# Six changes of order in a one-core decoder block, and its output projection's first weights asked for without the wait for the GDN inverse

## The reference

```
h = rmsnorm(x, g_mix);  proj = h @ w_in                      # GLA q,k,v,gate; GDN conv q,k,v; z; a,b
conv = silu(sum(xc[:, j:j + T] * gdn_conv_w[j] for j in range(4)))        # GDN q,k,v
o_a = gated linear attention(4 heads);   o_b = gated delta rule(8 heads)  # chunked for the prompt
x = x + concat(norm(o_a) * silu(gr), norm(o_b) * silu(z)) @ w_out
m = rmsnorm(mem, g_mem);  k = m @ w_k;  v = m @ w_v                       # memory of 256 rows
s = einsum('bthd,bmhd->bhtm', rmsnorm(x) @ w_q, k) * 512 ** -0.5          # 4 heads of 512
x = x + einsum('bhtm,bmhd->bthd', softmax(s), v) @ w_o                    # samples: cached k, v
x = x + (silu(h @ w_gate) * (h @ w_up)) @ w_down;   y = rmsnorm(x, g_final)
```

## Time and profile before

| | us |
|---|---|
| median of 3 runs | 1809.09 |
| lowest, highest run | 1808.67, 1809.23 |
| the profiled execution | 1807.64 |
| its span in the trace | 1805.9 |
| PE busy | 1766.5 (98%) |
| DVE, ACT, POOL busy | 1090.5, 763.2, 176.4 |

### The profile page before, as it was taken

The page is one execution under the profiler, slowest core; times in us unless marked ns, Lnnn a source line. Parts: engine busy times, 40 slices in busy tenths (PEclk is TensorE's granted clock), DMA queues, the critical chain, the costliest instruction groups (busy, mean ns, idle before and its releaser), DMA issues.

```text
span 1805.9 us, 34933 instructions
## 1 busy us (share of the span) xinstructions
PE 1766.5 (98%) x14223; PEld 1685.6 (93%) x14223; DVE 1090.5 (60%) x1501; ACT 763.2 (42%) x803; POOL 176.4 (10%) x179
## 2 busy tenths in 40 slices
PE   8999999999999999999999999999999999999997
PEld 6999999998999998786679999999999999999997
DVE  6888447756766676553366566665444566665443
ACT  5554546345733533343213444443333444433444
POOL 5000000001055000000015400000000000000231
PEclk9999999999999999999999999999999999999999
DMA  8455545552565679777935788885557888874553
GB/s 271 148 179 187 177 150 163 166 169 82 163 223 178 206 250 326 252 272 253 331 103 178 217 248 244 247 249 157 160 177 212 240 245 247 247 211 138 175 178 113
DMA packets 415130, 367.23 MB, mean 203 GB/s; under 512 B 11519, under 2 KB 374014, under 8 KB 414486
## 3 DMA queue, kind: packets, MB, share of 16 engines
q1 hardware_dynamic: 387368, 340.76, 61.2%
q10 hardware_dynamic: 27678, 25.26, 4.3%
HBM read 347.84 MB, written 18.35 MB: 203 GB/s over the span
## 4 chain that ended last, share of the span: by engine, by line
PE 89%; DVE 5%; ACT 2%; issue 1%; DMA 1%; POOL 1%; DVEq 0%; SPq 0%; ACTq 0%; POOLq 0%
PE ps L478 67%; PE ps L554 9%; PE ps L535 4%; DVE w_lo L457 2%; PE ps L1000 1%; PE ps L521 1%; PE ps L1123 1%; PE ps L1492 1%; ACT w_hi L450 1%; DMA gst<-in_state_gla_dram 1%; PE ps L1527 1%; DVE cacc L647 1%; DMA ring<-in_cache_mem_v_dram 1%; PE ps L1029 0%; PE ps L1536 0%
## 5 line engine op out<-in xcount | busy, mean ns | idle before, releaser
L450 ACT ACTIVATE w_hi<-raw 128x2048 fp32r<-128x2048 f32 (+1 forms) x285 | 512.2, 1797 | 913.6 <-PE ps L478 727.0
L457 DVE TENSOR_TENSOR w_lo<-raw,w_hi 128x2048 fp32r<-128x2048 f32 (+1 forms) x285 | 620.3, 2176 | 300.4 <-ACT w_hi L450 297.2
L478 PE MATMUL ps<-act_hi,w_lo 128*128 128x264 f32 x2560 | 733.9, 287 | 5.6 <-DVE w_lo L457 4.1
L478 PE MATMUL ps<-act_lo,w_hi 128*128 128x264 f32 x2560 | 726.5, 284 | 0.0
L478 PE MATMUL ps<-act_hi,w_hi 128*128 128x264 f32 x2560 | 726.1, 284 | 0.0
L478 PEld LDWEIGHTS ps<-act_hi,w_lo 128*128 128x128 f32 x2560 | 482.8, 189 | 9.6 <-issue 3.8
L478 PEld LDWEIGHTS ps<-act_lo,w_hi 128*128 128x128 f32 x2560 | 483.1, 189 | 0.5
L478 PEld LDWEIGHTS ps<-act_hi,w_hi 128*128 128x128 f32 x2560 | 480.5, 188 | 0.0
L478 PE MATMUL ps<-ff_hi,w_lo 128*128 128x264 f32 x704 | 201.5, 286 | 0.0
L478 PE MATMUL ps<-ff_hi,w_hi 128*128 128x264 f32 x704 | 200.4, 285 | 0.0
L478 PE MATMUL ps<-ff_lo,w_hi 128*128 128x264 f32 x704 | 199.7, 284 | 0.0
(11 more groups left out here) (454 smaller groups left out, 1967.0 us busy)
## 6 DMA issues: line engine op xcount, KB each, us to landing
raw<-in_w_in_dram SPq DMA_DIRECT2D x56, 1024.0 KB, 7.5
raw<-in_ffn_w_gate_dram SPq DMA_DIRECT2D x44, 1024.0 KB, 5.7
raw<-in_ffn_w_up_dram SPq DMA_DIRECT2D x44, 1024.0 KB, 5.7
raw<-in_ffn_w_down_dram SPq DMA_DIRECT2D x32, 768.0 KB, 4.9
raw<-in_ffn_w_down_dram SPq DMA_DIRECT2D x32, 640.0 KB, 6.2
raw<-in_w_out_dram SPq DMA_DIRECT2D x16, 1024.0 KB, 6.9
raw<-in_xa_w_q_dram SPq DMA_DIRECT2D x16, 1024.0 KB, 6.8
raw<-in_xa_w_k_dram SPq DMA_DIRECT2D x16, 1024.0 KB, 7.4
```

Source lines behind the costliest of these rows:

```text
L450: act.activation(w_part(ph, w_hi[b]), raw_part(ph, r, half), ACT.Copy)\
L457: dve.tensor_tensor(w_part(ph, w_lo[b]), raw_part(ph, r, half), w_part(ph, w_hi[b]), ALU.subtract)\
L478: mm = pe.matmul(ps[:, acc(ph, u), 0:ph.cols], w[b][:, k, :], v[:, kk + k, 0:ph.cols], start=first and k == 0 and m == 0, stop=last and k ...
```

## The change

There are seven edits. Six change an order, one takes a wait out.

1. The convolution's taps on DVE: the tap over the samples goes ahead of the one over the prompt, and each waits for its own predecessor, two instructions back.
2. w_out's unit (1, 0) is split in two halves of 8 tiles, each as soon as its part of the buffer is free; on DVE the low halves stand between the takes.
3. PE no longer waits for all takes of w_out ahead of the query projection. (Its first unit has waits of its own, tile by tile from k = 13.)
4. The two squares of the memory rows on ACT stand behind different splits (n = 1, 2), their root behind that of n = 3.
5. The sample queries are turned in the middle of their unit, and ACT copies them ahead of the split of that step.
6. The prompt's values use three accumulator banks instead of two, wait for their own rows of vm only, and the sample rows are turned first; DVE makes the low part of the next weights behind them.
7. SP's first loads of w_out no longer wait for `inv_ready`.

```
@@ new helpers for unit (1, 0) of w_out
+        def next_split_hi(act, m):
+            ph = PH["w_out"]
+            r, landed, half, b, n = unit_of(ph, 1, 0)
+            act.wait_ge(raw_landed[r][m], landed)
+            act.wait_ge(units_done, n + 2 * m - 1)
+            act.activation(w_hi[b][:, 8 * m:8 * m + 8, :], raw[:, r, 8 * m:8 * m + 8, half * P:half * P + P], ACT.Copy)\
+               .then_inc(hi_split if m else N["half_hi"], 1)
+
+        def next_split_lo(dve, m):
...
@@ wide_products; products has the same argument already
-        def wide_products(pe, ph, g, u):
+        def wide_products(pe, ph, g, u, middle=None):
...
+                if middle is not None and k == 1:
+                    middle()
@@ gdn on DVE
+                for j in range(CW):
+                    if j:
+                        dve.wait_ge(conv_ready, n * 8 + 2 * j - 1)
+                    if j == CW - 1:
+                        tap(j, of_samples, pre[:, b, 3 + T:3 + TT])
+                    else:
+                        tap(j, of_samples, cst[:, ds(n, 1), j * NB:(j + 1) * NB])
+                    if j:
+                        dve.wait_ge(conv_ready, n * 8 + 2 * j)
+                    else:
+                        dve.wait_ge(acc_free, ph.t0 + n + 1 + ACC_CREDIT)
+                    tap(j, of_prompt, pre[:, b, j:j + T])
@@ SP
             sp.wait_ge(srow_done, 1)
-            W(sp, "inv_ready", ready(LEVELS - 1, 0))
             for j in range(2):
                 load(sp, PH["w_out"], 0, j)
@@ PE, behind w_out
-            pe.wait_ge(acc_free, PH["x_q"].t0 + ACC_CREDIT)
@@ PE, prompt_values
-                if j >= 2:
-                    W(pe, "att_oe", j - 1)
+                if j % 4 == 0:
+                    rows_wait(pe, 1, j // 4)
+                if j >= 3:
+                    W(pe, "att_oe", j - 2)
                 for m in range(2):
-                    mm = pe.matmul(ps[:, 4 + j % 2, 0:T], vm[:, m, j * P:(j + 1) * P],
+                    mm = pe.matmul(ps[:, 4 + j % 3, 0:T], vm[:, m, j * P:(j + 1) * P],
@@ PE, the 48 units
+                query = QUERY_AT.index(n) if n in QUERY_AT else None
+                middle = None if query is None else lambda: turn_query(query)
...
-                if n in QUERY_AT:
-                    turn_query(QUERY_AT.index(n))
...
+            pe.wait_ge(rows_copied, 3)
+            for d in range(4):
+                mm = turn(ps[:, 7, d * P:(d + 1) * P], orow[:, d * P:(d + 1) * P])
+            mm.then_inc(rows_turned, 1)
             W(pe, "att_pT", XH)
-            rows_wait(pe, 1, 3)
@@ DVE, first units of w_out
             for u in range(4):
                 out_taken(0, u)
-                if u >= 2:
-                    split(ph, 1, u - 2)
+                if u == 1:
+                    next_split_lo(dve, 0)
+                if u == 2:
+                    next_split_lo(dve, 1)
+                if u == 3:
+                    split(ph, 1, 1)
```

More of the change, by code:

```diff
@@ L507, in half_split_lo @@
                               w_hi[b][:, k0:k0 + 8, :], ALU.subtract).then_inc(lo_split if h else N["half_lo"], 1)
+        def next_split_hi(act, m):
[6 more added lines that the diff above has]
+        def next_split_lo(dve, m):
+            ph = PH["w_out"]
+            r, landed, half, b, n = unit_of(ph, 1, 0)
+            if m:
+                dve.wait_ge(hi_split, n + 1)
+            else:
+                W(dve, "half_hi", len(HALF_ORDER) + 1)
+            dve.tensor_tensor(w_lo[b][:, 8 * m:8 * m + 8, :], raw[:, r, 8 * m:8 * m + 8, half * P:half * P + P],
+                              w_hi[b][:, 8 * m:8 * m + 8, :], ALU.subtract).then_inc(lo_split if m else N["half_lo"], 1)
         def half_products(pe, u, h, k_from=0, k_to=8):
@@ L1560, in _ @@
                     else:
-                        products(pe, ph, i, u, act_hi, act_lo)
+                        products(pe, ph, i, u, act_hi, act_lo, middle=middle)
                 else:
@@ L1564, in _ @@
                         pe.wait_ge(m_taken, KT + 2)
[L1565 to L1567 removed]
+                    wide_products(pe, ph, i, u, middle=middle)
                 for p in KEYS_AT.get(n, ()):
@@ L2080, in _ @@
             ph = PH["w_out"]
-            split(ph, 1, 0)
+            for m in range(2):
+                next_split_hi(act, m)
             split(ph, 1, 1)
@@ L2139, in _ @@
                     act.activation(q_rows[0:2 * NB, h % 2, :], ps[0:2 * NB, 6, :], ACT.Copy).then_inc(q_kept, 1)
+                if n < 3 * KT - 1:
+                    split(*unit_at(n + 2))
+                if n == 0:
+                    rms(2, TT, D)
+                if n in (1, 2):
+                    memory_squares(n - 1)
+                if n == 3:
+                    memory_rstd()
                 if n in (20, 24, 28, 32):
```

59 lines of the change are left out of this document (21 added, 38 removed).

## The result

With the change the kernel takes **1789.66 us** (median of 4 runs, 1788.85 to 1791.02), and before it 1808.88 (median of 4, 1808.08 to 1809.23): a ratio of 0.9895, 95% interval 0.9878 to 0.9912, or 19.2 us. The profiled execution took 1788.85, with a span of 1787.1 against 1805.9.

The account below looks back on a forecast made before the run. TensorE (PE), 89% of the chain that ended last, was taken as the bound, so only its holes counted; 4.8+1.7+1.6+1.4+4.0+5.5 = 19.0 us took the median from 1809.09 to 1790.1 us, range 1787.5 to 1795.0.

Parts of the forecast that it names:

- Taps: Convolution taps, gdn projection stage: a shorter DVE unit closes PE's holes, 4.8 us.
- First loop unit of w_out: Output projection: splitting the unit in halves removes PE's 1.5 us idle time, 1.7 us in starts.
- Wait for all takes: Ahead of the query projection: PE's 1.4 us idle for the last act_lo goes, 1.6 us in starts.
- Memory squares: ACT's squares spread over units 1 to 3: PE's 1.2 us idle time goes, 1.4 us of starts.
- Query rows: Query rows turned inside their unit, hole at unit 25: 2.4 us plus 1.55 of lower clock behind it, together 4.0.
- Rival 2: The lower clock comes back at another hole; 1.6 of the 4.0 us given back, 1791.7 us; chance 0.13.
- Prompt's values: Prompt values in three banks: PE and DVE run at their own pace, next products at 920.6, 5.5 us.
- Early weights: First w_out weights without the wait for the inverse: SP asks 2.5 us earlier, nobody waits for them, 0 us.
- Rival 3: Early w_out weights pay after all: 2.5 us more gain, 1787.6 us; chance 0.05.
- Rival 1: Taps gain nothing, as issue time, not completion, fills DVE's 5.77 us unit; 1794.9 us; chance 0.12, wholly or half.
- Rival 5: Each tap waits out the one just ahead, 1.0 us a pair instead of 0.77; 1811 us; chance 0.02.
- Rival 4: Slower: a denser TensorE in the gdn stage is held at the lower clock; 1817 us; chance 0.01.

Follow-up runs that it names:

- e1: Changed kernel with the convolution taps of before (prompt first, one wait for the pair); gdn stretch 150.16 us, span 1793.8 us.
- e2: e1 without the wait behind the last pair of taps; gdn stretch 148.39 us.
- e3: Changed kernel with the prompt tap ahead of the sample tap again, each wait still naming the tap two back; gdn stretch 145.45 us.
- e11: Changed kernel, same tap order, but each tap waits for the one just ahead; gdn stretch 149.95 us.
- e10: Changed kernel with w_out's first loop unit split whole, the wait for all takes back, both memory squares behind one split; stretches 71.32 and 26.28 us, half units 23.53.
- e6: Changed kernel with the query rows turned behind their unit again and copied behind the split; query projection stretch 148.70 us, +2.50.
- e8: Changed kernel with two banks instead of three for the prompt's values; stretch 22.61 us against 19.75.
- e9: Changed kernel with the prompt's values wholly as before (two banks, old waits, sample rows and weight halves in old places); stretch 25.82 us, +6.07.
- e7: Changed kernel with SP's wait for the inverse put back ahead of the first w_out weights; stretch 298.62 us against 298.60, span 1787.3.
- e5: Changed kernel with SP asking for the fifth and sixth batches of cached values ahead of slot 22 and 23 weights; 1786.84 us, ratio to before 0.9875.

## Why the prediction was right, point by point

The forecast was 1790.1 us (profiled 1788.6), the result 1789.66 (profiled 1788.85). The sum of 19.0 met 18.8, and that it met so closely is in part luck. The edits brought 18.5 us: the six gains of the table, 20.0, less the 1.5 of lower clock that stood behind unit 25 in the run of before. For them I had 17.45, the sum without its 1.55 for the clock. So the holes were worth 1.0 more than I said, and the term for the clock was worth nothing, since the profiled runs of before and after each have one stretch of 3.41 us. The 0.3 that is left lies in rows that belong to no edit.

- *Taps, 4.8: 5.19.* The holes hung on DVE's unit (e1), and its length on which tap each wait names (e2, e3, e11). One reading behind it was wrong in size: I took the 0.15 us between the end of a sample tap and the next prompt tap for the wait for completion. In the units behind the loop it is 0.03 (162.03 + 0.22 to 162.28); the rest is the register instruction that the wait holds back. That is why DVE gained 1.12 us a unit and not 0.7 to 0.9, which is cover and no time. The stretch's extra 0.4 lies in its first pair of units, which had 0.87 to give (6.00 and 6.58 from start to start before, 5.91 and 5.80 after) where I put 0.5; of the ten further pairs with 0.42 there were nine, at 0.47, and 0.12 in one last unit.
- *First loop unit of w_out, 1.7: 1.68,* and again in e10.
- *Wait for all takes, 1.6: 1.72. Memory squares, 1.4: 1.59.* Each hole costs about 0.1 to 0.2 more in starts than I put down; e10 gives 1.72 and 1.60.
- *Query rows, 4.0: 4.02 in the trace, and yet wrong in one step.* The hole was 2.50 (e6; I said 2.4). The other 1.55, "the granted clock falls behind it", I took as caused by the hole. Undoing the edit brought the hole back and not the lower clock. That term belongs to no edit.
- *Rival 2, the lower clock elsewhere (0.13).* It is what the profiled run of after shows: 1.60 given back at 850.88. Its chance was too low, for what I set against it, that the clock had not fallen after the 2.7 us wait, is one run's evidence on something that moves between runs of one program. Every profiled run pays it somewhere, so it should have stood in the sum as zero with a spread of 1.6 either way.
- *Prompt's values, 5.5: 5.79.* The tiles and the transposes take 0.44 + 13.63 = 14.07 us by their starts (the first transpose at 893.21, the next projection at 907.27), not the 14.35 of my sum. That three banks are needed holds (e8), and e9 gives the whole.
- *Early weights, 0: 0* (e7). The 0.27 us in that stretch are the wait for the GLA state, 0.2 in the waits of before, and stay away with the edit undone. Rival 3 falls.
- *Rival 1 and the rule behind it.* The taps gain 5.19 us, so rival 1 falls. It had something: 0.5 of the 5.77 us was issue and not completion, but issue that stood behind the waits, and so the change took that as well. The Trainium skill (VectorE: DVE Perf Modes, section "The DRAIN you can't avoid") says that the next operation starts only when the pipe is empty and that a semaphore adds nothing. The same section adds, which I left out, that a next operation starts earlier if it is not held. With that the rows agree, which overlap by up to 0.08 us where nothing is waited for. On the semaphore this case's runs disagree: e11 and the change issue the same operations in the same order and differ in which tap a wait names, and DVE needs 5.79 and 4.65 us a unit in the loop, 5.38 and 4.63 behind it.
- *Rival 5 (1811).* As an edit (e11) it costs 4.84 us and no more: a pair is 0.92 and not 1.0, three pairs pay and not four, and the wait behind the last pair, which is in the 5.77 I added them to, is gone. It would have ended near the old time of that stage, not 2 us above it.
- *Rival 4.* PE without a hole for 145 us in gdn was at a clock of 1.00 throughout. The five other gains are also in stretches at 1.00.

Open: what decides where the lower clock comes. The idle time just ahead of it does not decide alone (2.19 us at 740 in e6 and 2.7 in before's wait for values did not bring it, 2.63 in the changed kernel did), and the same program had it in one run and not in the other. I made no experiment that moves it at will.

## What to carry to other kernels

Holes at different places of a bound engine can be summed by their starts, each read from the view of waits and confirmed in the timeline; here six of them came in within 0.4 us each. On a chain of short dependent operations on one engine, let each wait name the operation two back, so that none waits for the one just issued. In a loop, look also at what else stands behind the wait: here a register instruction did, and cost as much again, and with the short independent operation first it was out of the way. Before you charge a stretch of lower clock to an edit, look at whether a second run of the same program has it at the same place. And where a wait ends on a DMA, read the issuing queue's timeline first: a request that stands behind another's wait looks like missing bandwidth, and moving one of two such requests only hands the wait to the next.

## What the hardware showed that I had not expected

- The granted clock fell to 0.50 for 3.41, 6.83 or 10.24 us, in every profiled run at least once ahead of the end, at places that change between runs of one program, and each 3.41 us costs 1.4 to 1.7. That would account for spans of one kernel that lie 2 to 3 us apart. The runs without a trace list only their mean granted clock, which goes with it: of the runs of before beside the experiments, the spans of 1809.9 and 1810.1 are at 0.993 and 0.994, those of 1806.0 to 1807.7 at 0.995 to 0.997.
- On DVE, a wait for the operation just issued adds 0.12 us from start to start, behind one of 128x8 as behind one of 128x256 (e11 against the change, behind the loop). A wait for the one two back adds nothing there.
- In a loop such a wait also holds back the register instruction that stands between it and the operation: 0.11 to 0.14 us more (0.77 against 0.66 a pair in before, 0.92 against 0.78 in e11), and 0.09 even for a wait two back when that operation is the long one (e3).
- DMA at a share of 1.05 (390 GB/s) for 30 us kept PE fed in e5, with requests for weights and cache values in turn.
